# Forming only the changed columns of each level in a blocked inverse (bidirectional RWKV-7 scan)

## The reference

```python
def step(s, inp):
    r_t, w_t, k_t, v_t, a_t, b_t = inp
    sa = jnp.einsum('bhij,bhj->bhi', s, a_t)
    s = s * w_t[:, :, None, :] + sa[..., None] * b_t[:, :, None, :] + v_t[..., None] * k_t[:, :, None, :]
    return s, jnp.einsum('bhij,bhj->bhi', s, r_t)
state, y = lax.scan(step, state, tuple(tm(t) for t in (r, w, k, v, a, b)), reverse=reverse)
```

## Time and profile before

| | |
|---|---|
| median of 3 runs | 2381.49 us (2381.33 to 2383.44) |
| profiled execution, its own time | 2385.74 us |
| its span, first to last instruction | 2383.9 us |
| granted TensorE clock, mean | 0.974 |
| TensorE busy (weight loads) | 91% (58%) |
| VectorE, ScalarE, GpSimd busy | 47%, 33%, 24% |
| matmuls of line 1796 (the levels), busy | 487.6 us of 11,520 records (all but `mt32`) |
| masked copies of line 1669 into TT, busy | 166.9 us of 400 |
| ScalarE copies of line 1604 into M, busy | 92.0 us of 240 |

### The profile page before, as it was taken

How to read it: one execution, slowest core, us unless ns; L and a number is a source line. 1 busy time by engine, 2 the same in 40 slices (tenths; PEclk the granted TensorE clock), 3 DMA queues, 4 the chain that set the end, 5 groups by cost and what they waited for, 6 DMA issues and landing times. The chain is left out here.

```text
span 2383.9 us, 55950 instructions
## 1 busy us (share of the span) xinstructions
PE 2177.3 (91%) x23884; PEld 1386.6 (58%) x23884; DVE 1121.6 (47%) x2213; ACT 794.9 (33%) x2048; POOL 580.0 (24%) x850
## 2 busy tenths in 40 slices
PE   7999999999799979999995898989898899989798
PEld 3556555354444435444443777777777777777543
DVE  4122122134746760021302666666666666666574
ACT  4111110143155522210001454545444444454432
POOL 0000000032023310000002444444444444444111
PEclk9999999999899989999997999999999999999899
DMA  9200002500137753555323334333333333333542
GB/s 350 108 27 27 24 21 103 206 36 18 38 87 195 202 159 123 165 179 168 115 71 103 81 105 131 93 87 93 88 88 88 85 90 95 83 94 79 188 141 106
DMA packets 306265, 258.49 MB, mean 108 GB/s; under 512 B 138465, under 2 KB 263649, under 8 KB 302562
## 3 DMA queue, kind: packets, MB, share of 16 engines
q1 hardware_dynamic: 306018, 254.92, 35.5%
HBM read 175.13 MB, written 79.69 MB: 107 GB/s over the span
## 5 line engine op out<-in xcount | busy, mean ns | idle before, releaser
L832 PE MATMUL ps<-xt,w_slab 128*128 128x512 f32 (+1 forms) x1344 | 534.3, 554 | 9.3 <-DVE xt L1052 9.3
L832 PEld LDWEIGHTS ps<-xt,w_slab 128*128 128x128 f32 x1344 | 253.1, 191 | 285.7 <-issue 256.6
L432 PE MATMUL ps<-h,fw_slab 128*128 128x512 f32 (+1 forms) x768 | 282.0, 527 | 2.1 <-ACT h L259 2.1
L1796 PE MATMUL ps<-M,AT 64*64 64x64 f32 x6400 | 270.9, 224 | 5.5 <-DVE M L1683 2.7
L1542 POOL TENSOR_TENSOR SP<-Q,decay 64x128 f32<-64x128 f32 x304 | 139.5, 459 | 465.8 <-DVE Q L1723 436.6
L1796 PEld LDWEIGHTS ps<-M,AT 64*64 64x64 f32 x6400 | 220.1, 135 | 49.0 <-issue 14.6
L1796 PE MATMUL ps<-TT,MT 64*64 64x64 f32 x5120 | 216.7, 224 | 20.3 <-ACT XT L1604 15.3
L432 PEld LDWEIGHTS ps<-h,fw_slab 128*128 128x128 f32 x768 | 145.7, 191 | 132.9 <-issue 125.4
L1796 PEld LDWEIGHTS ps<-TT,MT 64*64 64x64 f32 x5120 | 178.0, 135 | 51.3 <-issue 38.3
L1669 DVE COPY_PREDICATED TT<-mask,ps 128x256 f32<-128x256 int32 x400 | 166.9, 435 | 76.6 <-PE ps L1796 73.9
L1712 DVE STREAM_TRANSPOSE MT<-M 128x256 f32<-128x256 f32 x240 | 106.9, 445 | 148.0 <-ACT M L1604 145.6
(11 more groups left out here) (231 smaller groups left out, 2891.3 us busy)
## 6 DMA issues: line engine op xcount, KB each, us to landing
feat<-feature_scratch SPq DMA_DIRECT2D x160, 256.0 KB, 3.1
feature_scratch<-k_feats SPq DMA_DIRECT2D x64, 320.0 KB, 5.2
w_slab<-in_rwin SPq DMA_DIRECT2D x32, 512.0 KB, 5.7
feature_scratch<-k_feats SPq DMA_DIRECT2D x24, 640.0 KB, 6.8
k_feats<-in_modw SPq DMA_DIRECT2D x8, 1536.0 KB, 6.5
Q<-v_token_scratch SPq DMA_DIRECT2D x320, 32.0 KB, 2.6
Z<-v_token_scratch SPq DMA_DIRECT2D x320, 32.0 KB, 2.2
fgo<-in_modw SPq DMA_DIRECT2D x8, 1024.0 KB, 8.1
```

The lines of the kernel that those rows point to most:

```text
L432: mm = pe.matmul(ps[:, b0 + b, 0:n], wi[:, half, k, :], h0[:, k, a:a + n], start=k == 0, stop=k == KT - 1)
L832: mm = pe.matmul(ps[:, bank, 0:n], w[:, i % 2, k, :], src[:, k, a:a + n], start=k == 0, stop=k == KT - 1)
L1796: mm = pe.matmul(out[o, b, :], L[o, b, :], R[o, b, :], start=True, stop=True)
```

## The change

In a level only half of the columns change: for the forward direction the first k of every 2k columns, for the backward direction the last k. The new kernel forms these 32 of 64 columns of each block alone. `level` streams them with a stride (runs of k columns, `changed_in`) and writes them packed, 128 columns for the four blocks, in PSUM. The masked copy reads 128 packed columns and a packed mask and writes to the strided places of `TT[k]` (`changed`); ScalarE's copies into `M` do the same. Columns that a level doesn't change stay in `M` and `TT` as they are. To let one access pattern reach both directions, which start at different offsets, the buffers of `M` and `TT` get some columns more behind the four blocks. At the last level the changed columns of the transpose are written into `MT` itself (`x_cols`), so `XT` is gone and `sa` reads `MT`. All stationary operands, the transposes on VectorE, mask 0 and the order on every engine are as before. The input of masks shrinks from 6 x 256 to 256 + 5 x 128 columns.

The diff, cut to its core:

```diff
+NMASK = 256 + 128 * len(LEVELS)
...
-    maskf = sb("mask_in", [P, 6, 256])
-    mask = sb("mask", [P, 6, 256], I32)
+    maskf = sb("mask_in", [P, NMASK])
+    mask = sb("mask", [P, NMASK], I32)
...
-    AT, MT1, M, MT, XT = ([sb(f"{n}{s}", [P, B4, CK]) for s in two] for n in ("AT", "MT1_", "M", "MT", "XT"))
-    TT = {k: [sb(f"TT{k}_{s}", [P, B4, CK]) for s in two] for k in LEVELS}
+    AT, MT1, MT = ([sb(f"{n}{s}", [P, B4, CK]) for s in two] for n in ("AT", "MT1_", "MT"))
+    M_cols = [sb(f"M{s}", [P, B4 * CK + CK]) for s in two]
+    TT_cols = {k: [sb(f"TT{k}_{s}", [P, B4 * CK + 2 * k]) for s in two] for k in LEVELS}
+    blocks = lambda t: t[:, 0:B4 * CK].rearrange("p (b t) -> p b t", b=B4)
+    M, TT = [blocks(t) for t in M_cols], {k: [blocks(t) for t in TT_cols[k]] for k in LEVELS}
...
-    lev = lambda bank: ps[:, bank, 0:256].rearrange("p (b t) -> p b t", b=B4)
+    lev = lambda bank: ps[:, bank, 0:128].rearrange("p (b t) -> p b t", b=B4)
+    def changed(t, k):
+        by_dir = t[:, 0:B4 * CK + 2 * k].rearrange("p (d x) -> p d x", d=2)[:, :, 0:2 * CK]
+        return by_dir.rearrange("p d (i y) -> p d i y", y=2 * k)[:, :, :, 0:k]
+    def runs(t, k):
+        return t.rearrange("p (d i x) -> p d i x", d=2, x=k)
+    def changed_in(t, b, k, last):
+        return t.rearrange("p b (i y) -> p b i y", y=2 * k)[:, b, :, k if last else 0:2 * k if last else k]
+    def x_cols(t):
+        return t.rearrange("p b (h x) -> p (b h) x", h=2)[:, 1:7].rearrange("p (d h) x -> p d h x", d=2)[:, :, 0:3:2]
...
                 act.wait_ge(pa, count("first", j, cc, PA["m2"]))
-                act.activation(M[par(cc)][:], lev(4), ACT.Copy).then_inc(aa, 1)
+                act.activation(changed(M_cols[par(cc)], 2), runs(ps[:, 4, 0:128], 2), ACT.Copy).then_inc(aa, 1)
...
                 act.wait_ge(pb, count("second", j, cc, PB["mt32" if name == "xt" else name]))
-                act.activation((XT if name == "xt" else M)[par(cc)][:], lev(5), ACT.Copy).then_inc(ab, 1)
+                k = 32 if name == "xt" else int(name[1:])
+                act.activation(x_cols(MT[par(cc)]) if name == "xt" else changed(M_cols[par(cc)], k), runs(ps[:, 5, 0:128], k), ACT.Copy).then_inc(ab, 1)
...
-            def masked(o, i, m):
-                return v.copy_predicated(o, mask[:, m, :], i)
+            def masked(k, cc, bank):
+                lo = 256 + LEVELS.index(k) * 128
+                return v.copy_predicated(changed(TT_cols[k][par(cc)], k), runs(mask[:, lo:lo + 128], k), runs(ps[:, bank, 0:128], k))
...
                 v.wait_ge(aa, count("act_first", j, cc, AA["at1"]))
-                masked(flat(MT1[s][:]), flat(AT[s][:]), 0).then_inc(da, 1)
+                v.copy_predicated(flat(MT1[s][:]), mask[:, 0:256], flat(AT[s][:])).then_inc(da, 1)
                 v.wait_ge(da, count("dve_first", j, cc, DA["mt1"]))
-                v.transpose(flat(M[s][:]), flat(MT1[s][:])).then_inc(da, 1)
+                v.transpose(flat(M[s]), flat(MT1[s][:])).then_inc(da, 1)
...
                 v.wait_ge(pa, count("first", j, cc, PA[f"t{k}"]))
-                masked(flat(TT[k][par(cc)][:]), ps[:, 4, 0:256], 1 + LEVELS.index(k)).then_inc(da, 1)
+                masked(k, cc, 4).then_inc(da, 1)
...
                 v.wait_ge(aa, count("act_first", j, cc, AA["m2"]))
-                v.transpose(flat(MT[par(cc)][:]), flat(M[par(cc)][:])).then_inc(da, 1)
+                v.transpose(flat(MT[par(cc)][:]), flat(M[par(cc)])).then_inc(da, 1)
...
                 v.wait_ge(pb, count("second", j, cc, PB[f"t{k}"]))
-                masked(flat(TT[k][par(cc)][:]), ps[:, 5, 0:256], 1 + LEVELS.index(k)).then_inc(db, 1)
+                masked(k, cc, 5).then_inc(db, 1)
...
                 v.wait_ge(ab, count("act_second", j, cc, AB[f"m{k}"]))
-                v.transpose(flat(MT[par(cc)][:]), flat(M[par(cc)][:])).then_inc(db, 1)
+                v.transpose(flat(MT[par(cc)][:]), flat(M[par(cc)])).then_inc(db, 1)
...
-            def level(out, L, R, done):
+            def level(out, L, R, k, done, x=False):
...
-                        mm = pe.matmul(out[o, b, :], L[o, b, :], R[o, b, :], start=True, stop=True)
+                        mm = pe.matmul(out[o, b, :], L[o, b, :], changed_in(R, b, k, (b >= 2) != x)[o], start=True, stop=True)
...
-                level(lev(4), AT[s], M[s], pa)
+                level(lev(4), AT[s], M[s], 2, pa)
...
                 pe.wait_ge(da, count("dve_first", j, cc, DA["t2"]))
-                level(lev(4), MT1[s], TT[2][s], pa)
+                level(lev(4), MT1[s], TT[2][s], 2, pa)
...
                 pe.wait_ge(aa, count("act_first", j, cc, AA["m2"]))
-                level(lev(4), AT[s], M[s], pa)
+                level(lev(4), AT[s], M[s], 4, pa)
...
-                level(lev(5), MT[s], TT[4][s], pb)
+                level(lev(5), MT[s], TT[4][s], 4, pb)
...
                 pe.wait_ge(ab, count("act_second", j, cc, AB[f"m{k // 2}"]))
-                level(lev(5), AT[s], M[s], pb)
+                level(lev(5), AT[s], M[s], k, pb)
...
                 pe.wait_ge(db, count("dve_second", j, cc, DB[f"t{k}"]))
-                level(lev(5), MT[s], TT[k][s], pb)
+                level(lev(5), MT[s], TT[k][s], k, pb)
...
                 pe.wait_ge(db, count("dve_second", j, cc, DB["t32"]))
-                level(lev(5), TT[32][s], MT[s], pb)
+                level(lev(5), TT[32][s], MT[s], 32, pb, x=True)
...
-                    mm = pe.matmul(seq(7)[o, d, :], XT[par(c)][o, at(sub, d), :], Rs[sub][o, d, :], start=True, stop=True)
+                    mm = pe.matmul(seq(7)[o, d, :], MT[par(c)][o, at(sub, d), :], Rs[sub][o, d, :], start=True, stop=True)
...
-    smask = np.stack([np.repeat(m, 2, axis=1).reshape(P, 256) for m in tab_levels], axis=1)
+    first_cols = lambda k, d: [c for c in range(CK) if c // k % 2 == d]
+    level_cols = lambda m, k: np.concatenate([m[:, d, first_cols(k, d)] for d in (0, 0, 1, 1)], axis=1)
+    smask = np.concatenate([np.repeat(tab_levels[0], 2, axis=1).reshape(P, 256)] + [level_cols(m, k) for m, k in zip(tab_levels[1:], LEVELS)], axis=1)
...
```

## The result

The changed kernel takes 2653.6 us (median of 4 runs, 2625.9 to 2658.1) against 2382.5 for the kernel before (4 runs, 2381.3 to 2385.2): a ratio of 1.111, 95% interval 1.1045 to 1.1175. The profiled execution took 2655.8 us, with a span of 2654.0 against 2383.9, and a mean granted TensorE clock of 0.816 against 0.974. The forecast of 2348 was wrong, and so was its range to 2450: the rival in which TensorE loses its clock came true.

The account below looks back on a forecast made before the run. TensorE's in-order queue, with waits on copies, was taken to bound the scan; 79 spacings of 0.41 us (32) plus 2 for the fill took 34 from 2381.5, giving 2348 us, overall range 2330 to 2450.

Parts of the forecast that it names:

- the rival in which TensorE loses its clock: Whole scan: fewer streamed columns drop TensorE to 1.2 GHz; 2410 us for some periods (20%), 2869 for nearly all (18%).
- three waits that end last: Latent period: TensorE's in-order queue waits at m4 for XT and at mt32 for t32, late through VectorE's queue; 0.41 us saved.
- No gain in pace: Level groups: weight loads set the pace of 0.058 us a pair, so narrower streams gain nothing there.
- the pace rival: Level groups: pace follows the stream, pairs 27 ns closer, 1.3 us a period less; about 2295 us, chance 5%.
- The shorter ends: Last matmul of a level group: 32 fewer columns end it 0.026 us earlier, counted after mt32 and m4.
- XT copy 0.105: ScalarE's copy before m4: 128 instead of 256 columns, 0.105 us a period shorter, all on the path.
- Masked copy t32 0.137: VectorE's masked copy before mt32: 128 fewer columns, 0.137 us a period shorter, on the path.
- M16, 0.115 by way of Q: From m16 through its ScalarE copy to Q on VectorE: 0.146 us earlier, of which 0.115 a period was counted.
- Packed and strided forms at no price: Narrow copies: strides cost nothing on the deciding path, short runs have cover; the opposite rival 2375 us, chance 10%.
- The fill, 2 us: Before the scan's first r product at 1308.5: some ten exposed copies shorter by 0.1 us each, 2 us in all.
- The price of a low period, 6.6 us, and the point of decision at 5 periods: Scan: each period at 1.2 GHz costs 6.6 us more; 5 of the 80 periods eat the gain of 33.
- the partial case: Scan: 2 to 15 periods at 1.2 GHz give 2361 to 2447, say 2410 us; chance 20%.

Follow-up runs that it names:

- doubled streams: Changed kernel with each level matmul streaming its 32 columns twice, the second copy into PSUM columns nobody reads: 2359.0 us, ratio 0.989 to the kernel before.
- the five kernels of the table: Changed kernel; with two idle matmuls a period; levels 2, 4 streaming twice; levels 8 up twice; all twice: 2653.6, 2478.7, 2373.4, 2364.1, 2359.0 us.
- M alone: Kernel before with only ScalarE's four M copies cut to the 128 changed columns, streams still 64 columns: 2384.0 us, ratio 1.0001.

## Why the prediction was wrong, point by point

- *What bounds the scan* (TensorE's queue with three waits that end last): right. The period at the high level is 11.42, predicted 11.39 with 11.25 to 11.6.
- *No gain in pace; the weight load sets it*: right, at both levels (0.54 us a level, and 0.93 at 1.2 GHz, the same as with 64 columns). The 27 ns a pair of the pace rival show in no run; the pairs start 58 ns apart with 32 columns as with 64.
- *The shorter ends*, 0.026 twice: right in size. Between doubled and narrow streams at the high level lie 11.475-11.42 = 0.055. `m4` comes 0.11 earlier behind `r` (0.13 expected) and `mt32` 0.21 earlier behind `t2` (0.24).
- *XT copy 0.105*: 0.105. *Masked copy t32 0.137, plus what M and TT save elsewhere*: 0.155 for all masked copies.
- *M16, 0.115 by way of Q*: mis-sized. Alone it gives 0.06. M16's copy, the transpose and Q's start come 0.10 earlier, but the RBK that follows only 0.06; the first Q addition takes 0.28 in place of 0.24 there.
- *Packed and strided forms at no price*: right on the path (runs of 16 and 32 columns); the copy with runs of two takes 0.44 on VectorE, so that this one saved nothing. On ScalarE it is 0.290 for 0.277. Both lie under cover, as said.
- *GpSimd not named*: a miss. The prediction walked the latent period and carried it to all others; in the last period of a head pair the earlier start meets GpSimd's product and costs up to 0.38.
- *The fill, 2 us*: 4.0 with doubled streams (first `r` at 1304.5 for 1308.5).
- *The price of a low period, 6.6 us, and the point of decision at 5 periods*: right; 46 spacings of 79 were 15.9 us or longer, and 2348 + 46 x 6.6 = 2652 is close to what was measured, 2653.6.
- *The step that failed* is a term that the sum puts at nothing: it counts 79 spacings at the high level, 0.41 us shorter each, and nothing for the clock. Its ground was a clock of 1.00 in the steady period, and still with 7.62 of 10 us in flight; that is time in flight, and the runs show that the clock goes with what streams. In its place some 305 us were lost at the low level against 30 gained. The mechanism was among the rivals, with too little weight. The prediction saw that half of the columns vanish while the groups last as long, and it had the numbers, 4.2 and 2.1 us of streaming a period. It gave the forecast 47% and the clock 38% in two cases, 2 to 15 periods or nearly all. What came lies between the two. The range stopped at 2450, where the partial case did. The trace of before could not decide it, as it held no long stretch of groups with short streams; but it held a low start and a fall in mid-scan, and a case that costs 6.6 us a period against a gain of 0.4 deserved a range that reached it.
The Trainium skill ("TensorE: Matmul & The Clock Gate", section "Part 1: The HAM clock gate") has the clock follow how busy the engine has been. The runs part busy from streamed: a narrow period at the high level has TensorE in flight 10.60 of 11.41 us and does not keep its clock, the one in the earlier trace rows 10.81 of 11.80 and keeps it. Read as time in flight, the rule would have kept the clock; read as streamed columns, it goes with the order of the five kernels of the table.

## What to carry to other kernels

Look first at what sets the pace of a group of matmuls. Here it was the weight load, and a shorter stream behind it gained nothing but the last matmul's end and cost the clock of more than half of the scan. In such a case make the copies narrow and leave the stream as wide as it was, with unread columns if need be. Read the granted clock by slice for every change that takes columns from TensorE, and price one period at either level before anything else. Make the parts of such a change separately: here the copies were worth 24 us (2383.3 to 2359.0), and the narrow stream made with them cost 295.

## What was not expected of the hardware

- With the same copies and weight loads, halving the columns of 80 matmuls a period took the mean granted clock from 0.976 to 0.816; two idle matmuls of 256 columns a period gave back 175 us of the 295.
- The pairs of 64-column weight loads in a group start 0.058 us apart at 2.4 GHz and 0.10 at 1.2 GHz, whether 32 or 64 columns stream behind them.
- A masked copy of 128 columns in runs of two takes 0.44 us on VectorE, as long as one of 256 columns (0.435); in longer runs mostly 0.26 to 0.30.
- A 256-column masked copy in SBUF takes 0.89 us in place of 0.41 when a GpSimd product of 128x256 has started 0.1 us before it (seven times in the kernel with M alone); when the copy starts first, GpSimd's takes 0.91 in place of 0.67 (seven times in the kernel before).
